# Gate rows of the second mixer in tiles of 512 columns, and its spatial mixing set between the output tiles of the first branch

## What is computed

```python
h = rmsnorm(x) @ w_in                     # columns: q k v iq iw ik su sv ga gb
o_a = sparse attention (prompt and paged sample caches, 8 heads x 128)
u = gelu(su)                              # 1024 columns
v = rmsnorm(gelu(sv), g)                  # 1024 columns, a row statistic over all of them
s = einsum('gts,bcsgd->bctgd', tril(w_s), v) + b   # 8 groups of 128 columns, chunks of 128 tokens
o_b = u * s
merged = sigmoid(ga) * (o_a @ w_branch_a) + sigmoid(gb) * (o_b @ w_branch_b)
x = x + merged @ w_out
x = x + down(silu(conv(up(x))) ...)       # the feed-forward part, unchanged
```

## Time and profile before

| | us |
|---|---|
| median of three runs | 1443.95 (1439.81 to 1448.76) |
| the profiled execution | 1447.95 |
| its span, first to last instruction | 1446.3 |
| first value stretch (first image starts at 500.2) | 500 to 589 |
| second key stretch | 589 to 720 |
| second value stretch (starts at 720.5) | 720 to 812 |
| last side tile, first branch, spatial mixing | 812 to 903 |
| second branch | 903 to 955 |

### The profile page before, as it was taken

The page is one execution under the profiler, slowest core; times in us unless marked ns, Lnnn a source line. Parts: engine busy times, 40 slices in busy tenths (PEclk is TensorE's granted clock), DMA queues, the critical chain, the costliest instruction groups (busy, mean ns, idle before and its releaser), DMA issues.

```text
span 1446.3 us, 33244 instructions
## 1 busy us (share of the span) xinstructions
PE 1354.8 (94%) x14298; PEld 1208.4 (84%) x14298; DVE 796.3 (55%) x1143; ACT 415.9 (29%) x588; POOL 336.8 (23%) x427
## 2 busy tenths in 40 slices
PE   6989999999888999888999988999999999999997
PEld 4967699866777866678876887999999999999997
DVE  5278869854788500678600247343767667663221
ACT  4243323256211400011400222223433333332221
POOL 3613323446322000322000003212322222210000
PEclk8899999999999999999999998999999999999998
DMA  6414213232999899999799681243333333242232
GB/s 186 140 48 141 88 59 117 98 124 88 334 371 366 271 403 403 389 344 362 260 371 403 245 314 50 92 131 100 114 86 89 88 88 84 71 138 81 81 86 72
DMA packets 168573, 266.76 MB, mean 184 GB/s; under 512 B 19866, under 2 KB 131915, under 8 KB 159211
## 3 DMA queue, kind: packets, MB, share of 16 engines
q1 hardware_dynamic: 147227, 174.13, 35.7%
q0 software_dynamic: 14320, 78.22, 14.5%
q10 hardware_dynamic: 6880, 12.29, 2.5%
HBM read 240.30 MB, written 24.18 MB: 183 GB/s over the span
## 4 chain that ended last, share of the span: by engine, by line
PE 83%; DMA 4%; DVE 4%; ACT 3%; issue 3%; POOL 1%; SPq 1%; ACTq 0%; DVEq 0%; POOLq 0%
PE PS L1036 16%; PE PS L1037 15%; PE PS L1038 15%; PE PS L1312 5%; PE PS L1344 4%; PE PS L1423 3%; PE PS L1421 3%; PE PS L1422 3%; DMA R<-in_cache_v 3%; PE PS L1080 2%; PE PS L1213 1%; PE PS L1277 1%; PE PS L1081 1%; PE PS L1082 1%; DMA GAT<-ga_scratch 1%
## 5 line engine op out<-in xcount | busy, mean ns | idle before, releaser
L1036 PE MATMUL PS<-xn_hi,WH 128*128 128x288 f32 (+1 forms) x1424 | 432.4, 304 | 5.9 <-DVE xn_lo L1773 3.8
L1037 PE MATMUL PS<-xn_lo,WH 128*128 128x288 f32 (+1 forms) x1424 | 422.4, 297 | 4.7 <-issue 4.5
L1038 PE MATMUL PS<-xn_hi,WL 128*128 128x288 f32 (+1 forms) x1424 | 422.0, 296 | 0.0
L1036 PEld LDWEIGHTS PS<-xn_hi,WH 128*128 128x128 f32 (+1 forms) x1424 | 268.6, 189 | 24.2 <-issue 11.6
L1037 PEld LDWEIGHTS PS<-xn_lo,WH 128*128 128x128 f32 (+1 forms) x1424 | 269.1, 189 | 4.3 <-issue 4.2
L1038 PEld LDWEIGHTS PS<-xn_hi,WL 128*128 128x128 f32 (+1 forms) x1424 | 269.0, 189 | 1.5 <-issue 1.5
L606 DVE TENSOR_TENSOR WL<-W,WH 128x2048 fp32r<-128x2048 f32 (+2 forms) x73 | 154.7, 2119 | 183.5 <-ACT WH L1475 183.4
L1475 ACT ACTIVATE WH<-W 128x2048 fp32r<-128x2048 f32 (+2 forms) x81 | 144.8, 1788 | 110.8 <-PE PS L1423 74.8
L1515 ACT ACTIVATE STG<-PS 128x576 f32<-128x576 f32 (+2 forms) x44 | 23.3, 530 | 346.6 <-PE PS L1038 199.1
L661 POOL DMA_INDIRECT R<-in_cache_k,KROW x64 | 64.5, 1008 | 237.1 <-PE PS L1344 96.8
L1995 DVE STREAM_TRANSPOSE R<-R 128x2048 f32<-128x2048 f32 x42 | 95.8, 2295 | 20.5 <-PE PS L1312 17.7
(11 more groups left out here) (309 smaller groups left out, 2414.8 us busy)
## 6 DMA issues: line engine op xcount, KB each, us to landing
R<-in_cache_v SPq DMA_DIRECT2D x128, 512.0 KB, 7.1
W<-in_w_in SPq DMA_DIRECT2D x30, 1024.0 KB, 6.7
W<-in_w_up SPq DMA_DIRECT2D x44, 512.0 KB, 4.8
W<-in_w_down SPq DMA_DIRECT2D x16, 704.0 KB, 4.7
x_scratch<-xT SPq DMA_DIRECT2D x2, 2304.0 KB, 9.8
W<-in_w_branch_a SPq DMA_DIRECT2D x4, 1024.0 KB, 5.2
W<-in_w_branch_b SPq DMA_DIRECT2D x4, 1024.0 KB, 4.9
W<-in_w_out SPq DMA_DIRECT2D x4, 1024.0 KB, 5.0
```

Source lines behind the costliest of these rows:

```text
L1036: pe.matmul(out, hi[:, k, cols], x.hi_block(n)[:, tokens], start=first, stop=False)
L1037: pe.matmul(out, hi[:, k, cols], x.lo_block(n)[:, tokens], start=False, stop=False)
L1038: return pe.matmul(out, lo[:, k, cols], x.hi_block(n)[:, tokens], start=False, stop=last)
```

## The change

It does five things.

- **Row tiles of 512 columns.** `sv` is made in two halves of 512 columns, each in three tiles over two PSUM banks: rows 0 and 1, row 2, and row 3 with the samples. A step is now four matmuls of 512 columns; the samples use high and low tokens side by side (`gate_parts`), so 160 steps of three matmuls of 256 become 56 steps of four of 512.
- **Gelu and squares when a tile leaves PSUM.** ScalarE writes gelu to the staging buffer, VectorE sums its squares there; for the sample rows VectorE first adds the two partial sums.
- **Another table of places.** Behind a value page stands one step or none (11 of 16 pages have one), 44 steps in each value stretch, and the place `end` is gone.
- **Spatial mixing between `wa` tiles.** The transposes of its weights stand behind `wa` 2, two groups behind each of `wa` 3 to 6. ScalarE copies `wa` 0 to 3 out of PSUM without the gate; VectorE multiplies them later.
- **Other buffers and loads.** `ob`'s high part moves to the space of `xn1`, `GBT` to the space of `oa`'s low part, and the queue on SyncE is reordered.

```diff
     def steps(tile):
-        return KT if tile[0] == 'sv' else 2 * KT
+        return (12, 6, 10)[tile[2]] if tile[0] == 'sv' else 2 * KT
...
     def quota(place):
         if place[0] == 'V':
-            return 2 if place[3] % (4 if place[1] == 0 else 2) == 1 else 1
+            return int(place[3] not in (3, 6, 9, 12, 15))
...
+                parts = [lambda k: one(0, k)] + [[lambda k: one(1, k)], [], [both]][i]
+                todo = sum([part(k) for ks in (range(4), range(4, 8)) for part in parts for k in ks], [])
...
+                for n in range(4 * first, 4 * last):
+                    out, x, part, k, begin, end = todo[n]
+                    ready = split((kind, c, k // 4), 512, 4)
+                    ins = pe.matmul(out, x, ready[part][:, k % 4, :], start=begin, stop=end)
```

The loads on SyncE behind the second value stretch, in their new order:

```diff
-            side_loads('end')
             filled(sp, 'ot', 1, 3, 1)
-            rows_stored = len(side) // 2 - 1
+            sp.dma_start(SG, bass.AP(sg_norm_g.tensor, 0, [[0, P], [1, 1024]])).then_inc(S_("sg_in"), 16)
+            sp.dma_start(SB, bass.AP(sg_b.tensor, 0, [[0, P], [1, 1024]]).rearrange("p (g t) -> p g t", g=8))\
+                .then_inc(S_("sg_in"), 16)
+            sp.dma_start(WS, sg_w_s[0].rearrange("g t s -> t g s")).then_inc(S_("ws_in"), 16)
             for i in range(2):
-                sp.wait_ge(S_(f"side_stored{i}"), 16 * rows_stored)
+                sp.wait_ge(S_(f"side_stored{i}"), 8 * n_stored)
             sp.dma_start(SV[:, 0:4, :], sv_scr[0:4].rearrange("r p c -> p r c")).then_inc(S_("sv_back"), 16)
             sp.dma_start(SV[0:TS, 4, :], sv_scr[4, 0:TS, :]).then_inc(S_("sv_back"), 16)
+            sp.dma_start(obT, side_scr['su']).then_inc(S_("su_back"), 16)
             filled(sp, *side[-1])
             for i in range(4):
                 sp.dma_start(GAT[:, 2 * i:2 * i + 2, :], side_scr['ga'][:, 2 * i:2 * i + 2, :])\
                     .then_inc(S_(f"ga_back{i}"), 16)
...
+            filled(sp, 'wa', 7)
+            for i in range(4):
+                sp.dma_start(GBT[:, 2 * i:2 * i + 2, :], side_scr['gb'][:, 2 * i:2 * i + 2, :])\
+                    .then_inc(S_(f"gb_back{i}"), 16)
...
+            filled(sp, 'wb', 7)
             for i in range(4):
-                drained(sp, 'wb', 2 * i)
-                drained(sp, 'wb', 2 * i + 1)
                 sp.dma_start(xT1[:, 2 * i:2 * i + 2, :], x_scr[0][:, 2 * i:2 * i + 2, :])\
                     .then_inc(S_(f"x_back{i}"), 16)
```

The first branch on TensorE, and the late gate on VectorE:

```diff
+            for c in range(8):
+                project3(('wa', c), split(('wa', c // 2), 256), column(c), oa,
+                         (lambda k: pe.wait_ge(S_("oa_split"), k + 1)) if c == 0 else None)
...
+                if c == 3:
+                    pe.wait_ge(S_("sv_normed"), 1)
+                for g in {3: (0, 1), 4: (2, 3), 5: (4, 5), 6: (6, 7)}.get(c, ()):
+                    spatial(g)
...
+            def gated_late(c):
+                dve.wait_ge(S_(f"ga_back{c // 2}"), 16)
+                drained(dve, 'wa', c)
+                dve.tensor_tensor(mT[:, c, :], GAT[:, c, :], mT[:, c, :], ALU.mult)
```

288 lines of the change are left out of this document (174 added, 114 removed).

## The result

The changed kernel takes 1440.87 us (median of 20 runs), the kernel before 1449.72 (20 runs beside them): ratio 0.994, 95% interval 0.9926 to 0.9953. The forecast was 1425, range 1413 to 1437. So the change gives 8.9 us, less than half of the 19 forecast, and the time lies above the range. Of the 15.9 us between 1425 and 1440.87, 5.8 lie in the start of the sum: it set out from 1443.95, the median of three runs, and the twenty gave 1449.72. The profiled execution of after took 1440.35 us (span 1438.7).

A forecast was written before the change was run, and what follows sets the result against it. TensorE was taken to bound the kernel (83% of the chain that ended last), with the DMA setting the first value stretch. 0 - 4.7 - 0.3 - 16 + 2 = -19 us from 1443.95 gave 1425, range 1413 to 1437.

The forecast's parts named there:

- Second value stretch: Second group's value pages: TensorE sets the length, fewer, thicker steps save 4.7 us, bounds -7 and 0; the DMA's bytes fit.
- First value stretch: First group's value pages: the DMA sets the length, so no change, between -3.5 and +3.5 us.
- The keys "at nothing": Key stretches: they keep their 144 steps each, costed at nothing; only one load more or less would move there.
- The end of the second stretch and the tail: Last value page to `wb` 0 done: -0.3 us at the stretch's end, -16 us in the tail (bounds -20 and -6).
- Between `wb` and `out`: Before the state's transposes: the state lands late behind the residual's loads, +2 us, bounds 0 and +5.
- The values stay bound by the DMA: Rival, chance 0.18: second value stretch waits for pages and gains nothing, the first loses 3.5 us; 1433 us.
- TensorE falls to 1.2 GHz: Rival, chance 0.09: page waits in the value stretches halve TensorE's clock for two of eight images; 1467 us.
- More is gained: Rival, chance 0.14: first stretch free of the DMA (-3.5), second -5.5, tail gives 20, state in time; 1414 us.

The follow-up runs named there:

- kernel 4: The changed kernel with each page beyond the first eight asked for two pages later, as a ring of six would: 1453.43 us, ratio 1.0047.
- kernel 8: kernel 7 with steps 10, 10, 9, 15 and 15, 9, 9, 11 by image, so no side tile ends with an image's last page: 1427.18 us.
- kernel 11: kernel 8 with first-stretch chunks asked for behind its last page, their first split behind the image's copies, second-stretch chunk in its third image: 1429.01 us.
- kernel 5: The kernel before, with side steps of the second value stretch placed 32, 32, 22, 10 by image instead of 24 each: 1451.46 us, ratio 1.0013.
- kernel 3: The changed kernel with value-stretch steps 9, 9, 10, 16 and 16, 9, 9, 10 by image instead of 11 each: 1436.03 us, ratio 0.9923.
- kernel 7: The changed kernel with the edits of kernel 2, kernel 3 and kernel 6, and second-group pages asked for ahead of a weight chunk: 1427.51 us.
- kernel 2: The changed kernel with the first chunk of `su` asked for one image later, near the first value stretch's end: 1436.73 us, ratio 0.9929.
- kernel 6: The changed kernel with the second softmax copying probabilities out of PSUM before the side tile and two weight splits: 1438.61 us, ratio 0.9926.
- 12: The changed kernel with all eight spatial mixing groups put back behind the first branch's last tile: 1446.02 us, ratio 0.9992.
- kernel 13: The changed kernel with the first four `wa` tiles multiplied by the gate out of PSUM on VectorE, as before: 1449.85 us, ratio 1.0010.

## Why the forecast was wrong

**Second value stretch (-4.7, it gave -2.2).** The failed step is "The DMA must bring 56 pages ... 31.9 MB, 79 us at 402 GB/s: it fits". The work fell by 6.1, between the forecast and its bound of 7. But the sum over the stretch does not say when the bytes come. The DMA rests while the ring is full, as the windows of after show (262 and 319 GB/s while TensorE takes its first pages), and the one chunk stands among the pages of a ring that stores, by the estimate under kernel 4, 2.3 of them:

```profile
730.00:735.00 5.00, 5.00 (x68) 3.91 (x67) 2.77 (x5) 0.74 (x2) 0.00 (x0) 0.87 0.73 262
735.00:740.00 5.00, 5.00 (x100) 3.77 (x104) 0.00 (x0) 0.00 (x0) 0.00 (x0) 1.00 0.91 319
```

So 3.9 us of waiting came back: of the 4.8 us of page waits, 1.5 stand at 746.1, behind that rest, 0.6 at 758.9, and 2.7 at 767.3 and 771.6, behind the chunk. Kernels 8 and 11 show the last part, since the wait moves with the chunk. Kernel 5 shows in the kernel before that the same matmuls and bytes can wait more when they change places. That other places for the steps would cure it is not shown: kernel 3's 0.9 us stands behind a wait at the seam, and kernel 8, without that wait, has 4.4. Why the stretch never came under 90 us stays open in part: in kernel 7 the wait at the seam stood in the way, in 8 and 11 the pages again, and no kernel had both small.

**First value stretch (0, within 3.5; it took 8.2 more; by the means, 98.0 in five traces against 91.2 in two, 6.9).** The prediction named the mechanism ("the slower first two images leave the ring full, and the last two want pages faster than they come") and then took nothing for it: the failed step is "I take no change". Its upper bound held the added bytes alone. Order cost some 3.2 us (kernel 3) and the added chunk some 3.6 (kernel 2), each read from one trace, together 7.2 (kernel 7), and with even steps and no chunk among the pages the stretch is at TensorE's own length (kernel 11). The chunk's bytes alone are the prediction's 2.6 us; SyncE's 4.00 us at the request behind the pair may be part of its price.

**The keys "at nothing" (+1.8).** What moved was not a load but a split. Behind `su` 6 on ScalarE and VectorE there now stands the split of a new chunk, ahead of the copies that TensorE waits for: softmax 17.5 us in place of 15.2, and 12.3 with the copies first (kernel 6). The stage as a whole spreads from 129.4 to 133.7 us in after, 2, 3, 4, 12 and 13; its softmax part, 16.9 to 18.1 there against 15.2 and 15.8 in before and kernel 5, is clear of that. The prediction did not follow these two engines through the softmax.

**The end of the second stretch and the tail (-16.3, it gave -18.2).** Right. The new wait for the squares is 3.0 less 0.7 us, 2.3 against 2.2; from the last page to the first `oa_lo` it is 825.87 - 821.17 = 4.7 us against 4.5. There is no wait for the gate, which kernel 13 prices at 9.2 us, and none for the norms: done at 846.7, 8.7 us ahead of the first group at 855.43, where the forecast had 5.8. The groups went at 1.45 us in place of 1.63, 1.4 us of the difference.

**Between `wb` and `out` (+2, it gave +1.1).** Right: a wait of 1.5 us for the state, 7.1 us on its way.

**The rivals.** "The values stay bound by the DMA" had the place and the direction, and 1433 for a time: it gave the first stretch 3.5 us, which lost 8.2. "TensorE falls to 1.2 GHz" came in part: behind the wait of 5.7 us the clock was 0.67 for ten microseconds, two thirds of that at the lower level, and 0.94 over the stretch, against 0.98. With the waits gone it was 0.98 again (kernel 11, 500 to 585 us), so it went with the waits; what it cost beside them no run shows. The prediction misread its rows here: the window of the earlier trace rows, 555 to 560 us, stands behind waits of 1.4 and 0.2 us (553.3 and 554.7), and the wait of 2.5 us ended at 587.0, as TensorE's timeline of before shows:

```profile
553.31 0.65 PE L1344 MATMUL PS<-R,R 128*32 128x128 f32 x16 [1.40 <-DMA R<-in_cache_v]
...
587.05 0.65 PE L1344 MATMUL PS<-R,R 128*32 128x128 f32 x16 [2.52 <-DMA R<-in_cache_v]
```

So the fall is not kept for a long wait only. Nor does the length of a wait decide it: in after one of 1.5 us (746.1) was followed by a clock of 1.00 from 746 to 751 us, and three of 0.6 us stand in a window at 1.00 (581 to 591). The Trainium skill, page "TensorE: Matmul & The Clock Gate", section "HAM oscillation — how this bites in real kernels", says that a loop whose matmuls wait for DMA between bursts falls back again and again; here the clock fell behind some of the waits, and it did not last. In *More is gained* the sum comes to 1414.65, and its 5.5 us for the second stretch are worked out nowhere; nothing else rests on them.

**The sum.** -19 forecast, -7.6 in the traces (-8.9 by the medians): 8.2 for the first stretch, 2.5 for the second, 1.8 for the softmax and 1.4 ahead of the change, less 1.9 and 0.9 in the tail, are 11.1 of the 11.4 us between them. The rest of the miss in the time itself is the base: with before's median of twenty, 1449.72, the same -19 would have given 1430.7, still 10.2 us short.

## What to carry to other kernels

Where transfers run through a ring of buffers, compare the consumer's and the DMA's pace image by image, in spans no longer than the stock of the ring (its depth less what is under way), and not by the sum of bytes over a stretch: what the DMA rests in dear spans is not there in cheap ones, and a load of 1 MB among pages of 512 KB showed as a wait of 2 to 3 us, some 12 us behind its request, in the stretches that waited for pages. Before a load is added or a step moved, follow every engine that the step touches through the next seam, since a split of 2 us ahead of a copy or a scaling showed as waits of 3.4 and 5.4 us on TensorE, and of 15.5 where its chunk came late. And taking bytes out of a bound stretch paid here only as far as the next one had room for them (kernel 11).
